# The five sums over partitions of a decoder block: two products of ones with a high and a low part, and no wait for their end

## What is computed

```python
def rmsnorm(x, g):
    return x * lax.rsqrt(jnp.mean(x * x, axis=-1, keepdims=True) + EPS) * g

def layernorm(x, g, b):
    mu = jnp.mean(x, axis=-1, keepdims=True)
    var = jnp.mean(jnp.square(x - mu), axis=-1, keepdims=True)
    return (x - mu) * lax.rsqrt(var + EPS) * g + b

def swiglu(h, w_gate, w_up, w_down):
    return (jax.nn.silu(h @ w_gate) * (h @ w_up)) @ w_down

# hs: 272 x 2048
hs = hs + 0.5 * swiglu(rmsnorm(hs, ffn1_norm), ...)         # 2048 -> 5632 -> 2048
u = rmsnorm(hs, mix_norm) @ w_in + b_in                     # five groups of 1024 channels
y_sc = b_sc * causal_dwconv(c_sc * v_sc, conv_sc_w)         # width 3
z = causal_dwconv(a_cf * sigmoid(g_cf), conv_cf_w) + conv_cf_b   # width 31
y_cf = silu(layernorm(z, ln_cf_g, ln_cf_b))
hs = hs + concat([y_sc, y_cf]) @ w_out
hs = hs + 0.5 * swiglu(rmsnorm(hs, ffn2_norm), ...)
out = rmsnorm(hs, final_norm)[16:]
```

## Time and profile before

| | us |
|---|---|
| median of 3 runs | 1851.29 |
| lowest and highest of them | 1850.97, 1871.83 |
| the profiled execution's own time | 1850.03 |
| its span, first to last instruction | 1848.2 |
| PE busy in the span | 1837.1 (99%), granted clock 0.999 |
| PEld, DVE, ACT busy | 1792.3 (97%), 1085.9 (59%), 902.1 (49%) |
| HBM traffic | 342.29 MB, mean 185 GB/s |

### The profile page before, as it was taken

How to read it: one execution, slowest core, us unless ns; L and a number is a source line. 1 busy time by engine, 2 the same in 40 slices (tenths; PEclk the granted TensorE clock), 3 DMA queues, 4 the chain that set the end, 5 groups by cost and what they waited for, 6 DMA issues and landing times.

```text
span 1848.2 us, 34879 instructions
## 1 busy us (share of the span) xinstructions
PE 1837.1 (99%) x14421; PEld 1792.3 (97%) x14421; DVE 1085.9 (59%) x1219; ACT 902.1 (49%) x1151; POOL 5.8 (0%) x16
## 2 busy tenths in 40 slices
PE   9999999999999999999999999999999999999998
PEld 9999999999999999999999999999999999988886
DVE  7555555555554455469899887555555555544454
ACT  6434343343443444359888665444444444444443
POOL 1000000000000000000000000000000000000000
PEclk9999999999999999999999999999999999999999
DMA  7655555555567777755655566666666666666664
GB/s 225 194 180 174 178 179 174 181 174 177 179 175 178 177 178 179 179 174 172 190 183 177 178 213 189 195 194 191 193 193 193 192 193 193 215 193 190 193 188 136
DMA packets 283359, 342.29 MB, mean 185 GB/s; under 512 B 10639, under 2 KB 223985, under 8 KB 283152
## 3 DMA queue, kind: packets, MB, share of 16 engines
q1 hardware_dynamic: 282672, 340.44, 62.1%
q10 hardware_dynamic: 320, 0.53, 0.1%
q0 software_dynamic: 288, 0.19, 0.0%
HBM read 339.02 MB, written 2.10 MB: 185 GB/s over the span
## 4 chain that ended last, share of the span: by engine, by line
PE 99%; DMA 0%; DVE 0%; ACT 0%; SPq 0%; issue 0%; DVEq 0%
PE ps L522 29%; PE ps L520 29%; PE ps L521 28%; PE ps L632 4%; PE ps L634 4%; PE ps L633 4%; DMA m_rows<-in_meta_tokens 0%; PE ps L482 0%; PE ps L650 0%; PE ps L657 0%; PE ps L536 0%; ACT o_tok L932 0%; SPq L366 0%; ACT sq_tok L742 0%; DVE res L1184 0%
## 5 line engine op out<-in xcount | busy, mean ns | idle before, releaser
L522 PE MATMUL ps<-x_hi,w_class__lo 128*128 128x272 f32 (+2 forms) x3200 | 901.6, 282 | 0.0
L520 PE MATMUL ps<-x_hi,w_class__hi 128*128 128x272 f32 (+2 forms) x3200 | 900.8, 281 | 0.1
L521 PE MATMUL ps<-x_lo,w_class__hi 128*128 128x272 f32 (+2 forms) x3200 | 900.3, 281 | 0.0
L947 DVE TENSOR_TENSOR w_class__lo<-raw,w_class__hi 128x1024 fp32r<-128x1024 f32 x400 | 489.3, 1224 | 422.3 <-ACT w_class__hi L718 420.9
L718 ACT ACTIVATE w_class__hi<-raw 128x1024 fp32r<-128x1024 f32 x400 | 424.3, 1061 | 564.8 <-PE ps L522 564.4
L521 PEld LDWEIGHTS ps<-x_lo,w_class__hi 128*128 128x128 f32 x3200 | 602.3, 188 | 0.0
L520 PEld LDWEIGHTS ps<-x_hi,w_class__hi 128*128 128x128 f32 x3200 | 601.5, 188 | 0.5 <-PE ps L536 0.5
L522 PEld LDWEIGHTS ps<-x_hi,w_class__lo 128*128 128x128 f32 x3200 | 601.6, 188 | 0.0
L947 DVE TENSOR_TENSOR w_same__lo<-raw,w_same__hi 128x1024 fp32r<-128x1024 f32 x200 | 244.1, 1224 | 256.9 <-ACT w_same__hi L718 256.8
L718 ACT ACTIVATE w_same__hi<-raw 128x1024 fp32r<-128x1024 f32 x200 | 211.6, 1060 | 314.4 <-PE ps L522 170.0
L522 PE MATMUL ps<-a_hi,w_same__lo 128*128 128x272 f32 x640 | 183.4, 287 | 0.0
(11 more groups left out here) (167 smaller groups left out, 1504.6 us busy)
## 6 DMA issues: line engine op xcount, KB each, us to landing
raw<-in_ffn_w_up SPq DMA_DIRECT2D x176, 512.0 KB, 3.5
raw<-in_ffn_w_down SPq DMA_DIRECT2D x176, 512.0 KB, 4.8
raw<-in_ffn_w_gate SPq DMA_DIRECT2D x175, 512.0 KB, 3.5
raw<-in_w_in SPq DMA_DIRECT2D x80, 512.0 KB, 3.6
raw<-in_w_out SPq DMA_DIRECT2D x32, 512.0 KB, 4.8
x_tok<-in_x SPq DMA_DIRECT2D x4, 512.0 KB, 7.7
gain_tok<-in_final_norm SPq DMA_DIRECT2D x1, 1024.0 KB, 4.6
out_y<-o_tok SPq DMA_DIRECT2D x2, 512.0 KB, 2.8
```

The costliest lines, as they stand in the source:

```text
L520: pe.matmul(dst, w_high, act_high, start=first, stop=False)
L521: pe.matmul(dst, w_high, act_low, start=False, stop=False)
L522: return pe.matmul(dst, w_low, act_high, start=False, stop=last)
L947: dve.tensor_tensor(w_lo, raw_rows(phase, s), w_hi.bitcast(F32), ALU.subtract).then_inc(lo_ready, 1)
```

## The change

The sum tile is split in a high and a low part of type fp32r, which take the place of the two tiles of `sq`. VectorE does that after the last addition: one copy and one subtraction for each of the five sums, and once a copy of `ones` to fp32r. PE then adds two fp32r matmuls into the same bank where one float32 matmul stood, and waits for the split (`sum_low`) in place of the additions. It no longer waits for the end of its own sum. The waits of VectorE for the sum's end stay.

```diff
+        sq_at = nc.sbuf_base
         sq = sb("sq", [P, 2, T])
...
+        ones_r = sb("ones_r", [P, P], F32R)
...
+        sum_hi = at("sum_hi", sq_at, [P, T], F32R)
+        sum_lo = at("sum_lo", sq_at + 4 * T, [P, T], F32R)
...
+        nth_sum = {"start": 1, "down1": 2, "ln_mean": 3, "ln_var": 4, "out_cf": 5}
...
+            def sum_over_partitions(dst, toks):
+                pe.matmul(dst, ones_r[:, :], sum_hi[:, toks], start=True, stop=False)
+                return pe.matmul(dst, ones_r[:, :], sum_lo[:, toks], start=False, stop=True)
+
             def square_sums(norm, phase):
-                pe.wait_ge(sum_ready[norm], 5 if norm == "start" else KD)
-                pe.matmul(ps[:, 7, 0:width[phase]], ones[:, :], sq_sum[:, tokens(phase)],
-                          start=True, stop=True).then_inc(stats_done[norm], 1)
-                pe.wait_ge(stats_done[norm], 1)
+                pe.wait_ge(sum_low, nth_sum[norm])
+                sum_over_partitions(ps[:, 7, 0:width[phase]], tokens(phase)).then_inc(stats_done[norm], 1)
...
                 if b == 6:
-                    pe.wait_ge(ln_added, KS)
+                    pe.wait_ge(sum_low, nth_sum["ln_mean"])
                     pe.wait_ge(emptied, banks_before("out_sc", 1))
-                    pe.matmul(ps[:, 0, SEQ:2 * SEQ], ones[:, :], ln_sum[:, :],
-                              start=True, stop=True).then_inc(ln_mean_done, 1)
-                    pe.wait_ge(ln_mean_done, 1)
+                    sum_over_partitions(ps[:, 0, SEQ:2 * SEQ], slice(0, SEQ)).then_inc(ln_mean_done, 1)
...
+            def split_sum(total, toks, n):
+                dve.tensor_copy(sum_hi[:, toks], total).then_inc(sum_high, 1)
+                dve.wait_ge(sum_high, 1 + nth_sum[n])
+                dve.tensor_tensor(sum_lo[:, toks], total, sum_hi[:, toks].bitcast(F32),
+                                  ALU.subtract).then_inc(sum_low, 1)
...
+                if t == KD - 1:
+                    dve.wait_ge(sum_ready[norm], KD)
+                    split_sum(sq_sum[:, toks], toks, norm)
...
+                            if c == KS - 1:
+                                dve.wait_ge(ln_added, KS)
+                                split_sum(ln_sum[:, :], slice(0, SEQ), "ln_mean")
...
                     dve.tensor_tensor(ln_sum[:, :], y_f[:, 0, :], y_f[:, 1, :], ALU.add).then_inc(ln_var_sum, 1)
+                    dve.wait_ge(ln_var_sum, 1)
+                    split_sum(ln_sum[:, :], slice(0, SEQ), "ln_var")
...
+            dve.tensor_copy(ones_r[:, :], ones[:, :]).then_inc(sum_high, 1)
+            dve.wait_ge(sum_ready["start"], 5)
+            split_sum(sq_sum[:, :], ALL, "start")
```

More of the change, by code:

```diff
@@ L236, in build @@
         first_loaded = [sem("first_loaded0"), sem("first_loaded1")]
+        sum_high, sum_low = sem("sum_high"), sem("sum_low")
         ones_set, ident_zero, ident_set = sem("ones_set"), sem("ident_zero"), sem("ident_set")
         par_turned, par_ready, x_turned = sem("par_turned"), sem("par_ready"), sem("x_turned")
+        nth_sum = {"start": 1, "down1": 2, "ln_mean": 3, "ln_var": 4, "out_cf": 5}
         gain_of = {"start": "ffn1", "down1": "mix", "out_cf": "ffn2"}
@@ L671, in layernorm_sums @@
                 if b == 6:
-                    pe.wait_ge(ln_added, KS)
+                    pe.wait_ge(sum_low, nth_sum["ln_mean"])
                     pe.wait_ge(emptied, banks_before("out_sc", 1))
-                    pe.matmul(ps[:, 0, SEQ:2 * SEQ], ones[:, :], ln_sum[:, :],
-                              start=True, stop=True).then_inc(ln_mean_done, 1)
-                    pe.wait_ge(ln_mean_done, 1)
+                    sum_over_partitions(ps[:, 0, SEQ:2 * SEQ], slice(0, SEQ)).then_inc(ln_mean_done, 1)
                 if b == 10:
-                    pe.wait_ge(ln_var_sum, 1)
+                    pe.wait_ge(sum_low, nth_sum["ln_var"])
                     pe.wait_ge(emptied, banks_before("out_sc", 2))
-                    pe.matmul(ps[:, SET, SEQ:2 * SEQ], ones[:, :], ln_sum[:, :],
-                              start=True, stop=True).then_inc(ln_var_done, 1)
-                    pe.wait_ge(ln_var_done, 1)
+                    sum_over_partitions(ps[:, SET, SEQ:2 * SEQ], slice(0, SEQ)).then_inc(ln_var_done, 1)
                 if b == 7:
```

## The result

| | kernel before | changed kernel |
|---|---|---|
| median of 21 runs, us | 1851.16 | 1868.67 |
| lowest, highest | 1850.58, 1871.87 | 1850.37, 1870.22 |
| runs below 1860 | 16 of 21 | 7 of 21 |
| profiled execution, us (span) | 1850.03 (1848.2) | 1869.56 (1867.7) |
| granted clock in it | 0.999 | 0.999 |

A forecast was written before the change was run, and what follows sets the result against it. PE was taken to bound the kernel, with 99% of the chain. 3.86 us leave and 1.16 enter, 2.70 gross; less waits of 0.48 and 0.09, 2.1 us net: from median 1851.29 to 1849.2, range 1847.0 to 1853.0.

The forecast's parts named there:

- So a microsecond of PE time that goes is a microsecond of the kernel: Whole kernel: PE holds 99% of the chain, so work added elsewhere costs only where PE comes to wait for it.
- the clock is out of it: Whole span: the clock was granted at 0.999 of 2.4 GHz, so it was left out of the forecast.
- 1.3 us: Spread of the three executions nearest to each other, added at both ends of the range of cases.
- Gross gain of the first two sums: "start" and "down1", 272 wide: each sum frees 0.79 us of PE's stream and brings in two products of 0.12 us.
- The split's 0.80 us: VectorE in out_sc: the copy and the dependent subtraction push the low part that follows by 0.80 us.
- The wait at block 6, 0.48: out_sc: the low part has 0.32 us margin and comes 0.80 late, so PE newly waits 0.48 us.
- Block 11, 0.09: out_sc: the second layer norm split delays this block's low part, so PE waits 0.09 us for it.
- Nothing later is late: Behind block 11: L1150, which had stood 1.85 us waiting for the sum, lets VectorE catch up; no further wait.
- Slower: Rival at the five sums: ten products at 0.39 us each plus waits of 0.57; 0.6 us more, 1851.9; chance 0.08.
- No gain: Rival: PE's stream resumes no earlier, or the time is given back at a later wait; 1851.3 us; chance 0.12.
- VectorE paces both sums: Rival at the layer norm: PE gets nothing from "ln_mean" and "ln_var"; 1.64 us less, 1849.7; chance 0.15.

The follow-up runs named there:

- the second profile of the changed kernel: The changed kernel timed once more as it is, beside the kernel before on one chip: 1869.15 us, 4 of 4 runs above 1860 us.
- the partial one: The kernel before with the change at the sums of "start" and "down1" alone, the three 256-wide sums left as before: 1849.98 us against 1850.92, ratio 0.9981.
- the first comparison: First timing of follow-up kernels beside the kernel before, on one chip; there the kernel before had 3 of 25 runs above 1860 us.
- each half of the change alone: Changed kernel with its five waits put back: 1851.18 us, ratio 1.001; kernel before with its five waits taken out, one float32 product kept: 1870.28 us, ratio 1.0092.

## Why the forecast was wrong

**The step that failed** is "So a microsecond of PE time that goes is a microsecond of the kernel", on which the last sum rests (1850.03 less 2.1). The sum has terms for what leaves and enters the stream and for new waits, and none for the pace of the other matmuls, which it took as given; "the clock is out of it" was right and was not enough. The 1.8 us around the span did stay. The pace of the 256-wide stages is not given: it has two values, and the wait that was removed was the main thing that put the longest of these stages at the faster one. Its absence costs 18.3 us in the executions that stay slow. None of the rivals had this. The sign of it stood in the runs before: 1871.83 lay 20 us above the other two, and I widened the range by "1.3 us" of scatter and left that run aside as an outlier. One of three was a heap, not noise.

**What the profiles show of the turn.** Seventeen profiles hold 50 sums of 256 columns. Rates are the mean step of the ten matmuls ahead of a sum, and of twenty starting five behind it:

| | fast, then fast | fast, then slow | slow, then fast | slow, then slow |
|---|---|---|---|---|
| PE waits for the sum's end | 9 | 1 | 6 | 3 |
| the stream goes on | 0 | 13 | 7 | 11 |

With the wait, 15 of 19 sums are left at the fast rate; without it 7 of 31. No sum in an unbroken stream left the fast rate as it was, one float32 product as little as two fp32r ones. Away from the sums and the added breaks the rate mostly holds, but it changed at nine places in these profiles. Four are at the first block of out_cf (three to fast, one to slow). Two lie two blocks further on, both to slow. One is at the head of gu2 without a break, to slow. Two stand right behind PE's wait of 0.38 us for the low part of block 6, both to slow, where three other profiles with the same wait stayed fast. So a sum is where the rate turns most often, but neither a sum nor a wait for PE's own end is needed. In sixteen of the seventeen profiles (all but the one with a break at each group) the rate of gu2 agrees with the heap of the execution's time. That is shown. Over executions the third norm's wait stands for the same: with it 8 of 48 are upper in four variants of the changed kernel, without it and without a break behind it 51 of 65 in six kernels (the changed one twice, as one). Left out of both counts is the kernel without the third sum (4 of 5). What in PE keeps the rate, and what of a break decides it, was not found; the addresses were tried and are not it.

**The terms that can be checked where the rate is not in play.**

- Gross gain of the first two sums: 1.10 us forecast; out_sc begins 1.36 us earlier (1.18 in the second profile of the changed kernel, 1.26 in the partial one). Right, a little low. That start moves by up to 0.66 us between profiles with the same changes ahead of it, so one sum by itself says more. From its start to the second matmul behind it, a 272-wide sum takes 0.91 us in the kernel before, 0.695 with two products and the wait, 0.59 with one product and no wait, 0.37 with both changes. The products give 0.21, the missing wait 0.32, together 0.53; two sums make 1.07.
- The split's 0.80 us: 0.78. The wait at block 6, 0.48: 0.38 where PE runs fast, in five profiles; none where it runs slow and arrives later.
- Block 11, 0.09: no pause is seen there in either profile of the changed kernel.
- "Nothing later is late": wrong. At the first block of out_cf PE waits 0.65 us (0.28 in the second profile). The trace before showed a margin of 0.3 us there, and the forecast has PE there 1.6 us earlier; the prediction followed VectorE to block 11 and did not look on to this place.
- From out_sc to the third norm's sum the table has +3.05: the rate gives 32 of 36 blocks x 24 x 4.44 ns = 3.41, the wait at out_cf 0.65, and the two sums -1.06: together 3.00.
- In the upper heap the saving is 2.35 us, near the 2.1 of the forecast. On the chip of the first comparison the kernel before has its upper runs at 1871.7, each half of the change alone at 1870.3. No upper execution of the kernel before was profiled, so it is not shown that the terms behind the 2.35 are those of the forecast.

**The rivals.** "Slower" forecast 0.6 us more by ten products of 0.39 us each: they run at 0.12. It had the sign right and the mechanism wrong. "No gain" gives nearly the right number for the lower heap, where the changed kernel is no better than the one before, and one of its two reasons, the time given back at a later wait, is there at out_cf. What else uses up the 2.7 is argued: the wait at block 6, and the slow rate in the output projection, which costs 3.4 us if it holds throughout. No lower execution of the changed kernel was profiled. "VectorE paces both sums" falls with block 11.

## What to carry to other kernels

A kernel whose runs fall in two heaps has a state, and a change is to be judged by how it moves the share of the heaps: profile one execution of each, and compare the steps of the busiest stream before any wait. Engines at 99% busy and full clock can still run the same matmuls 4% slower; a count of matmuls per window shows it in one line. And a wait that costs a third of a microsecond may decide at which pace the stream behind it runs: take it out alone, and run it often enough to count.

## What the runs showed of the hardware

- A stream of fp32r products, 256 columns wide, each with its own 128x128 weights, runs at 113.3 or at 117.8 ns, at a granted clock of 1.00 in both; it keeps either through the 469 or 486 us from the third sum to the end of gu2. The Trainium skill, "TensorE: Matmul & The Clock Gate", section "Back-to-back issue gap", gives N/2.4 + 2.5 ns as the gap of a single matmul, which is 109 ns for 256 columns as an estimate by that page, and for a stream with weight loads only values at 128 and 512 columns; both rates here lie above the 109 ns.
- With 272 columns the mean step is 123.5 ns in every profile; two rates were not seen there.
- A float32 product of 256 columns stands as two records 0.215 us apart. With no wait behind it the next product starts 0.25 us after its first record, and the one after that 0.30 us later; with the wait the next product starts after 0.65 us.
- With a break at the head of every group of gu2, the fast and the slow rate alternated from group to group for 400 us.
